# Scan mixer of a two-layer model: step size folded into the decay exponent, skip accumulated by TensorE

## The reference, cut to what matters

```
def ssd_scan(x, dt, A, Bm, Cm):
    X = (x.astype(jnp.float32) * dt[..., None]).reshape(b, c, l, G, R, P)
    a = (dt * A).reshape(b, c, l, G, R).transpose(0, 1, 3, 4, 2)
    a_cs = jnp.cumsum(a, axis=-1)
    CB = jnp.einsum("bclgn,bcsgn->bcgls", Cc, Bc)
    scores = CB[:, :, :, None] * jnp.exp(segsum(a))
    y_diag = jnp.einsum("bcgrls,bcsgrp->bclgrp", scores, X)
    decay_states = jnp.exp(a_cs[..., -1:] - a_cs)
    states = jnp.einsum("bclgn,bcgrl,bclgrp->bcgrpn", Bc, decay_states, X)
...
    y_off = jnp.einsum("bclgn,bcgrpn,bcgrl->bclgrp", Cc, prev, jnp.exp(a_cs))
    return (y_diag + y_off).reshape(b, L, H, P)
...
    dt = jax.nn.softplus(dt.astype(jnp.float32) + dt_bias.astype(jnp.float32))
    A = -jnp.exp(A_log.astype(jnp.float32))
    y = ssd_scan(xs, dt, A, Bm, Cm) + xs * D_skip[:, None]
    y_a = rmsnorm(y * jax.nn.silu(z), ssd_norm_w)
```

## Time and profile before

| what | value |
|---|---|
| median of three runs | 4057.89 us (4051.12 to 4060.33) |
| the profiled execution, whole | 4057.06 us |
| its span in the trace | 4055.4 us |
| the mixer stage in it | from 2311.0 to 2446.6 us |
| VectorE busy in the whole span | 2587.6 us (64%) |
| GpSimd busy in the whole span | 1207.5 us (30%) |
| instructions | 53218 |

### The profile page before, as it was taken

One profiled execution on the slowest core, in us unless ns is written; L12 is line 12 of the kernel. 1 busy time (PEld: TensorE's weight loads), 2 busy tenths in 40 slices (PEclk: granted clock), 3 DMA queues, 4 the chain that ended last, 5 costly groups with the idle time before them and its releaser, 6 DMA issues. The chain is left out here.

```text
span 4055.4 us, 53218 instructions
## 1 busy us (share of the span) xinstructions
PE 3707.8 (91%) x19688; PEld 3144.3 (78%) x19688; DVE 2587.6 (64%) x4367; ACT 1828.5 (45%) x3365; POOL 1207.5 (30%) x1139
## 2 busy tenths in 40 slices
PE   7889777799999989999999987879999999999888
PEld 6757656577788878878887786768799999999867
DVE  6569874434677766613476477867567776776666
ACT  3135455414433334521344356764555455555444
POOL 1422220023111100211234461100366666666400
PEclk9869888899999999999999998989999999999989
DMA  4222301255367664531134585765311111111064
GB/s 149 80 82 81 120 14 37 95 187 183 111 232 255 240 251 146 170 124 69 58 121 152 179 193 115 147 176 185 91 35 53 37 49 47 40 50 43 22 222 146
DMA packets 348287, 485.37 MB, mean 120 GB/s; under 512 B 45356, under 2 KB 218957, under 8 KB 344045
## 3 DMA queue, kind: packets, MB, share of 16 engines
q1 hardware_dynamic: 311116, 371.33, 29.0%
q0 software_dynamic: 34608, 106.45, 9.0%
q10 hardware_dynamic: 2304, 4.20, 0.3%
HBM read 337.43 MB, written 144.47 MB: 119 GB/s over the span
## 5 line engine op out<-in xcount | busy, mean ns | idle before, releaser
L119 PE MATMUL hg_acc<-l_first_ws,l_XT 128*128 128x256 f32 x2880 | 359.6, 285 | 0.0
L119 PEld LDWEIGHTS hg_acc<-l_first_ws,l_XT 128*128 128x128 f32 x2880 | 348.8, 192 | 0.0
L119 PE MATMUL hg_acc<-l_XT,hg_ws 128*128 128x512 f32 x1440 | 343.1, 394 | 0.0
L119 PEld LDWEIGHTS hg_acc<-l_XT,hg_ws 128*128 128x128 f32 x1440 | 266.7, 189 | 52.4
L4632 POOL TENSOR_TENSOR hg_DD<-hg_BB 128x256 f32<-128x256 f32 x224 | 173.9, 776 | 260.3 <-PE hg_pA L4391 133.4
L4489 DVE TENSOR_TENSOR hg_DD<-hg_Q,hg_DD 128x256 f32<-128x256 f32 x224 | 204.3, 912 | 73.3 <-ACT hg_DD L4560 73.2
L119 PE MATMUL even_bank<-l_first_ws,l_XT 128*128 128x512 f32 x888 | 206.2, 390 | 3.2 <-PEq L852 1.9
L119 PE MATMUL even_bank<-even_ws,l_XT 128*128 128x512 f32 x876 | 204.4, 390 | 0.0
L119 PEld LDWEIGHTS even_bank<-l_first_ws,l_XT 128*128 128x128 f32 x888 | 166.2, 188 | 40.7 <-issue 6.0
L119 PEld LDWEIGHTS even_bank<-even_ws,l_XT 128*128 128x128 f32 x876 | 163.9, 188 | 33.9
L119 PE MATMUL am_g_acc<-l_XT,am_ws 128*128 128x512 f32 x768 | 179.1, 396 | 8.6 <-ACT am_stage L2077 8.6
(11 more groups left out here) (741 smaller groups left out, 9346.9 us busy)
## 6 DMA issues: line engine op xcount, KB each, us to landing
l_first_raw<-in_odd_w_in SPq DMA_DIRECT2D x64, 512.0 KB, 5.5
l_first_raw<-in_even_w_in SPq DMA_DIRECT2D x16, 1024.0 KB, 5.5
l_room_tiles<-hidden SPq DMA_DIRECT2D x63, 256.0 KB, 8.5
da_first_X<-q_k_hi POOLq DMA_DIRECT2D x24, 512.0 KB, 8.0
da_first_X<-q_k_lo POOLq DMA_DIRECT2D x24, 512.0 KB, 13.7
l_room_tiles<-y_even SPq DMA_DIRECT2D x45, 256.0 KB, 7.2
ffn_y<-in_w_ffn_down SPq DMA_DIRECT2D x22, 512.0 KB, 4.6
weight_sums_w_ffn_down<-ffn_y SPq DMA_DIRECT2D x11, 1024.0 KB, 4.0
```

The costliest lines, as they stand in the source:

```text
L119: mm = pe.matmul(out, lhs(p, k), rhs(q, k), start=start and i == 0, stop=stop and i == n - 1, skip_group_check=skip)
```

## The change

The skip's product no longer comes from GpSimd. Once, at the start of the stage, GpSimd makes `skips`, 16 tiles of 128x128, each the identity times the D_skip of a head. `diagonal` issues for every head two matmuls in place of one: skips times x, then scores times x accumulated on it. The tiles Xd and XD, their GpSimd instructions and GpSimd's addition into Y go; `gate` waits for VectorE's own addition. For the scores to hold the step size, ln(dt) is added to the exponent's bias NA, and DS is multiplied by dt; that takes one clamp and two small products or sums on VectorE and one logarithm on ScalarE in `even_inputs`.

```
@@ even_inputs
+                    if i == MIX_AT + 14:
+                        mixer.join_steps(dve)
@@ MixerStart
+LEAST_STEP = 1e-37
...
         dve.tensor_tensor(self.work[2], self.work[1], self.work[0], ALU.subtract).then_inc(self.argument, 1)
+        dve.wait_ge(self.argument, 2)
+        dve.tensor_scalar(self.work[0], self.flat[0], LEAST_STEP, None, ALU.max).then_inc(self.argument, 1)
...
         act.activation(self.flat[2], self.work[2], ACT.Exp).then_inc(self.exps, 1)
-        act.wait_ge(self.exps, 6)
+        act.wait_ge(self.argument, 3)
+        act.activation(self.work[1], self.work[0], ACT.Ln).then_inc(self.exps, 1)
+        act.wait_ge(self.exps, 7)
+
+    def join_steps(self, dve):
+
+        dve.wait_ge(self.exps, 7)
+        self.link(dve.tensor_tensor(self.flat[2], self.flat[2], self.flat[0], ALU.mult))
+        self.link(dve.tensor_tensor(self.flat[4], self.flat[4], self.work[1], ALU.add))
@@ ssd_mixer, SyncE
                 def load_inputs(c):
-                        sp.wait_ge(xk, c - NS + 1)
+                        sp.wait_ge(yd, c - NS + 1)
@@ GpSimd
-                by_dt(0)
+                pool.tensor_tensor(skips[:, :, :], ident[:, :].unsqueeze(1).to_broadcast([P, H2, P]),
+                                   hd[:, 3, :].unsqueeze(2).to_broadcast([P, H2, P]), ALU.mult).then_inc(skipped, 1)
                 for c in range(NCH):
                     if c + 1 < NCH:
+                        pool.wait_ge(x_ld[c % NS], (c // NS + 1) * DMA)
                         if c:
                             pool.wait_ge(ns, c)
-                        pool.tensor_tensor(heads(Xs[:, :]), heads(Xd[:, :]), bc64(pr[:, DS, c, :]), ALU.mult).then_inc(xs, 1)
+                        pool.tensor_tensor(heads(Xs[:, :]), heads(X[c % NS][:, 0:X2]), bc64(pr[:, DS, c, :]), ALU.mult).then_inc(xs, 1)
                         pool.wait_ge(xs, c + 1)
-                    pool.tensor_tensor(heads(XD[:, :]), heads(X[c % NS][:, 0:X2]), bc64(hd[:, 3, :]), ALU.mult).then_inc(xk, 1)
-                    pool.wait_ge(xk, c + 1)
-                    if c + 1 < NCH:
-                        by_dt(c + 1)
                     if c in (2, 4):
                         attention.load_parts(pool, c // 2 - 1)
-                    pool.wait_ge(yt, c + 1)
-                    pool.tensor_tensor(Y[:, c % 2, :], Y[:, c % 2, :], XD[:, :], ALU.add).then_inc(y1, 1)
-                    pool.wait_ge(y1, c + 1)
@@ TensorE
                 def diagonal(c):
-                    pe.wait_ge(xd, c + 1)
+                    pe.wait_ge(x_ld[c % NS], (c // NS + 1) * DMA)
                     if c:
                         pe.wait_ge(yt, c)
+                    else:
+                        pe.wait_ge(skipped, 1)
                     for h in range(H2):
                         if h % 4 == 0:
                             pe.wait_ge(sc, G2 * c + h // 4 + 1)
-                        mm = pe.matmul(pYd[:, h, :], SC[:, h, :], Xd[:, h * P2:(h + 1) * P2], start=True, stop=True,
-                                       skip_group_check=True)
+                        x = X[c % NS][:, h * P2:(h + 1) * P2]
+                        pe.matmul(pYd[:, h, :], skips[:, h, :], x, start=True, stop=False, skip_group_check=True)
+                        mm = pe.matmul(pYd[:, h, :], SC[:, h, :], x, start=False, stop=True, skip_group_check=True)
                     mm.then_inc(yd, 1)
@@ VectorE
                 def gate(c):
-                    dve.wait_ge(y1, c + 1)
+                    dve.wait_ge(yt, c + 1)
```

More of the change, by code:

```diff
@@ L3479, in ssd_mixer @@
         SC = pl.sb("SC", [P, H2, P])
-        Xd = pl.sb("Xd", [P, X2])
+        skips = pl.sb("skips", [P, H2, P])
         Xs = pl.sb("Xs", [P, X2])
-        XD = pl.sb("XD", [P, X2])
         Y = pl.sb("Y", [P, 2, X2])
@@ L3500, in ssd_mixer @@
         rounded = pl.sem("mask_rounded")
-        xd = pl.sem("dt_x_ready")
         xs = pl.sem("decayed_x_ready")
-        xk = pl.sem("skip_ready")
-        y1 = pl.sem("skip_added")
+        skipped = pl.sem("skips_ready")
         cbS = pl.sem("CB_ready")
@@ L3581, in _ @@
             def _(pool):
[L3582 to L3587, removed]
                 pool.tensor_copy(hidden[:, :], neg[:, :]).then_inc(rounded, 1)
```

## The result

The changed kernel takes 4071.78 us, the median of five runs (4067.74 to 4079.26), against 4052.93 us for the kernel before on the same chip (five runs, the three shown among them). The ratio is 1.0043, 95% interval 1.003 to 1.0055: slower by some 17 us, with 12 to 22 in the interval. The profiled execution took 4067.74 us; it was the fastest of the five. Each ratio in this document is against executions of the kernel before taken beside it, and leaves out two executions, one of e4 (6263.81 us) and one of e9 (4582.19 us), in which the granted clock was 0.581 and 0.768 where it is about 0.95 in all others.

The account below looks back on a forecast made before the run. The prediction took the stage as a loop through all engines with TensorE having the least room. Inner steps +13.1, chunk 0 +3.7, step 0 to 1 +2.5 and the end -2.1 sum to +17.2 us: 4075, range 4065 to 4083.

Parts of the forecast that it names:

- All up to `diagonal` stays, D+10.62: Inner chunk, counted from D, the start of `keys`: work before `diagonal` keeps its uncontended timing, `diagonal` starting 10.62 us later.
- `diagonal` 7.36 us, a step 17.98: Inner chunks on TensorE: 64 pairs at 0.115 us make steps of 17.98 us; six of them add 13.1 us.
- near bounds: TensorE pair price between 0.111 and 0.120 us, 3.6 to 3.8 us a chunk, giving +16.3 to +18.5 us.
- Chunk 0, +3.7: First chunk: `diagonal` grows by 3.7 us from its 32 added pairs.
- Step 0 to 1, +2.5: Step without a turn: `diagonal` starts at D+8.75, so the step is 16.11 us against 13.57, +2.5 us.
- The end, -2.1: End of the stage: `gate` no longer sits behind a norm of 3.45 us, now 1.28, saving 2.1 us.
- `skips` hides behind the first chunk: Start of the stage on GpSimd: the one `skips` product, estimated at 3.8 us, may take 9 before anyone waits; cost nothing.
- `even_inputs` costs nothing: Added logarithm, table load and small VectorE instructions hide under TensorE's matmuls; uncovered they would cost 2.5 us once.
- Rival 1: Faster: TensorE's gaps take in the pairs and a 14.1 us loop through other engines decides; -12.0 us, 4046; chance 0.05.
- rival 2: About no change: half the added pairs run in waits for scores; -8 to +8 us, 4058 in the middle; chance 0.09.
- Rival 3: Slower by more: GpSimd's Xs falls on VectorE's norm, delaying `turn` and TensorE; +28 us, 4086; chance 0.09.
- the 0.8 us a chunk: Cost of 32 pairs by the skill's issue floor near 25 ns, weighed against 3.4 us by its weight-load figure.

Follow-up runs that it names:

- e4: Kernel before without GpSimd's XD and its addition into Y, so the skip is left out; Xd and Xs stay: ratio 0.9957, stage 124.3 us.
- e9: Kernel before with VectorE's addition, XD made after the gate and turn early, step size not folded, Xd kept: ratio 0.9973, stage 125.4 us.
- e1: Changed kernel without the 16 skip matmuls of each chunk, skips tiles still made, skip missing from the result: ratio 0.9962, stage 123.6 us.
- e2: Changed kernel with every skip matmul issued twice, so the skip is added twice: ratio 1.0102, stage 179.5 us.
- e5: Changed kernel with turn(c-2,1) moved on TensorE ahead of sums(c,3): ratio 1.0035, stage 149.3 us.
- e6: Changed kernel with the skip given back to GpSimd (XD and addition), leaving only the step size's folding: ratio 0.9997, stage 134.9 us.
- e8: Changed kernel with the skip as two 512-column matmuls of the plain identity over XD, made by GpSimd a chunk ahead: ratio 1.0008, stage 136.4 us.
- e10: Like e7, but with turn(c-2,1) back behind off_diagonal: ratio 0.9991, stage 127.4 us.
- e7: Changed kernel without skip matmuls: GpSimd makes XD a chunk ahead, VectorE adds it, off-diagonal product and turn earlier: 4040.83 us, ratio 0.9962.
- e3: Changed kernel with skip matmuls over 32 of a head's 64 columns, half the skip left out: ratio 1.0101, stage 181.1 us.

## Why the prediction was right

The forecast was 4075 us, with a range of 4065 to 4083, and 4071.78 was measured. As a difference it was +17.2 us; the interval gives +12 to +22, and the stage grew by 16.3. The cause it named is the one that e1 and e2 show: TensorE's own order ends the step, and the added pairs lengthen it in full. Term by term:

- **All up to `diagonal` stays, D+10.62.** Measured D+10.64. Right.
- **`diagonal` 7.36 us, a step 17.98.** Measured 7.14 and 17.79. The price of a pair was 0.1116 us, the lower of the near bounds and not the 0.115 taken: the unbroken run of chunk 0 was a little slower than the ones behind it. Six steps grew by 106.6 - 94.7 = 11.9 us, not 13.1. With 0.1116 us for all 64 pairs the prediction's own sum gives +15.5 us. Its near bounds, +16.3 to +18.5, put another price on the added pairs only; on all 64, as in the sum, they would be +15.2 and +19.8.
- **Chunk 0, +3.7.** Its sum of outputs starts 18.12 us into the stage, before 13.97: +4.15. The pairs are 3.57 of it. The other 0.6 lies ahead of `diagonal`: the granted clock in the stage's second 5 us was 0.91, and 1.00 in the kernel before. I take that for chance of the execution. e4, which has no skip matmuls and no `skips`, shows the same 0.6 (14.62), and so do e5 and e6; e1 shows none (14.01), nor does e2, which has more matmuls than the changed kernel. The same kernel was not profiled twice for it. No term of the forecast has this 0.6, so that the measured 16.3 is nearer to the 17.2 than the terms are by themselves: that much is luck.
- **Step 0 to 1, +2.5.** 15.99 - 13.57 = +2.4.
- **The end, -2.1.** From the last sum of outputs to the end of the stage it was 13.36 us before and is 11.19: -2.2.
- **`skips` hides behind the first chunk.** The product took 3.60 us (an estimate of 3.8), nobody waited. Right.
- **`even_inputs` costs nothing.** One table load of 1.28 and a logarithm of 0.31 came; the moves behind them are 5.44 us apart as before.
- **What was missed.** VectorE's product of the state (L3793 before) took 1.91 us in every chunk before, beside GpSimd's Xd, and takes 1.22 now. A duration that was the same seven times looked like the operation's own, and was contention. The norm therefore starts at D+2.9, not D+3.6. It is worth nothing here, since `turn` stands behind `new_state` until D+4.76. The wait of VectorE for pYd is 3.8 us rather than 3 for another reason: `gate` starts at D+7.93, 0.74 us earlier than before without its wait for GpSimd, and the last score at D+12.42 in place of D+13.17. GpSimd and VectorE in the kernel before, three collisions:

```profile
2354.99 1.90 POOL L3586 TENSOR_TENSOR ssd_Xd<-ssd_early_first,ssd_first_pr 128x1024 f32<-128x1024 f32 x1 [6.38 <-PE ssd_pYd L3648]
2356.06 1.91 DVE L3793 TENSOR_TENSOR ssd_ST<-ssd_ST,ssd_first_pr 128x1024 f32<-128x1024 f32 x1
...
2377.89 1.90 POOL L3601 TENSOR_TENSOR ssd_XD<-ssd_X,ssd_first_hd 128x1024 f32<-128x1024 f32 x1
2379.12 1.75 DVE L3757 TENSOR_TENSOR ssd_Y<-ssd_Y,ssd_Z 128x1024 f32<-128x1024 f32 x1
...
2434.64 2.34 POOL L3608 TENSOR_TENSOR ssd_Y<-ssd_Y,ssd_XD 128x1024 f32<-128x1024 f32 x1 [9.27 <-DVE ssd_Y L3789]
```

Of that contention the Trainium skill ("SBUF — State Buffer", section "Who interferes with whom") says that a VectorE instruction with two SBUF inputs contends with a GpSimd instruction that reads SBUF, and that one with at most one SBUF input does not. The rows agree: the product of the state took 1.91 and now takes 1.22 us, the norm 3.05 and 1.28, the gate 1.75 to 1.81 in four of eight chunks and now 1.22 (1.39 in chunk 0, beside Xs), while the sum of outputs, with one input in PSUM, took 1.22 us in both kernels. The same section says that issue order decides who waits. One row does not bear this out: the last norm (3.45 us) is listed at 2434.60, 0.04 us ahead of the addition, and it is the norm that waited.

Rival 1 and rival 2, that gaps take in the pairs, fall with e1 and e2: nothing was hidden. Rival 1's own sum was also loose: TensorE's order without the pairs takes 10.62 + 3.68 = 14.30 us, more than the loop of 14.1 that the rival went by (e1 measured 14.2), and step 0 to 1 was left out of its -12.0. The short gap between matmuls of few columns that the Trainium skill gives ("TensorE: Matmul & The Clock Gate", section "Back-to-back issue gap") isn't seen with a weight load before each, and the 0.8 us a chunk that the prediction worked out from it was never a price for these pairs: the section calls the gap isolated and too small where weight loads come between. The 0.112 us is that page's 107 ns for a load of 128 columns (section "LDWEIGHTS (loading the stationary operand)") and a little more. That the load sets the price, and not another fixed cost of a pair, no run here can tell. Rival 3 falls with the norms of 1.28 us.

The six steps from chunk 1 to chunk 7, which the chance of chunk 0 does not touch, give the bookkeeping: 94.7 us before, 9.4 less without XD and the addition on GpSimd (e4), another 0.1 less without Xd (e1), and 21.4 more with the pairs on TensorE (changed), 106.6.

## What to carry to other kernels

Work that is moved off an engine for the contention it makes has to land where there is idle time in the loop, not on the engine that ends the step: the same skip cost 28 us on TensorE as 32 small pairs, 13 as four wide ones (e8 against e1), and 3.8 on VectorE between the scores and pYd, the move of the off-diagonal product included (e10 against e1), each with `turn` in its old place. The 28 and the 3.8 each hold the 0.6 us of chunk 0 that e1 was spared. With the early turn the version with VectorE's addition (e7) takes as long as no skip at all with the old order, 84.9 us for the six steps against 85.2 in e1; e1 was not run with an early turn, so what the addition costs there is not known. Before a product goes to TensorE as scaled identities, count its weight loads: a pair with 128x128 weights cost 0.112 us here over 32 columns as over 64. And a duration that never varies may still hold contention that never varies.

## What was not expected of the hardware

Matmuls over fewer columns made the kernel slower. In e3 the skip ran over 32 of 64 columns, at the same 0.112 us a pair, and with the engine never idle for 8.8 us the granted clock fell from 1.00 to its lower level, in the `diagonal` shown after 6 us, and it fell so in every chunk; pairs then took 0.21 us, and the steps from chunk 1 on 21.4 to 21.6 in place of 17.8. In e2, with half again as many pairs in a row and all of 64 columns, it stayed at 1.00 from chunk 1 to the end of the last `diagonal`. What decides this was not tried further.
